# Regrouping the adaLN front of a fused block: modulation weights in stages of 256 shift and 256 scale columns, two blocks without ctx begun early, ctx turned later

## The chip, the cores and the metric

The kernel runs on one core of a Trainium2 chip. The metric is the device time of one execution in microseconds (us), lower is better. The engines are TensorE (PE; PEld is its weight load), VectorE (DVE), ScalarE (ACT), GpSimd (POOL) and SyncE (SP), which here only issues DMAs.

## The reference

Two transformer-like blocks in float32, sequence 512, width 2048. Only the start of the first one is touched:

```python
sc, scc = silu(c), silu(c_ctx)
shift, scale, gate       = split(sc  @ w_ada + b_ada, 3)      # w_ada: 2048 x 6144
shift_c, scale_c, gate_c = split(scc @ w_ada + b_ada, 3)
hc = rmsnorm(ctx, g_pre) * (1 + scale_c) + shift_c            # 256 x 2048
zc = hc @ w_in[:, :XBC_W + DT_W]                              # 4096 + 64 columns
hx = rmsnorm(x, g_pre) * (1 + scale) + shift                  # 512 x 2048
zx = hx @ w_in                                                # 12352 columns
xbc = silu(dwconv(z[..., :4096]));  ...                       # scans, MLP, w_out, second block
```

The 4096 `xbc` columns of `w_in` are sixteen blocks of 256. Blocks 0 to 11 (xh and B) are also needed for ctx; blocks 12 to 15 (C) are needed for x alone, as the last layer takes no output from ctx.

## The kernel before

Every float32 product is made from two fp32r parts (high by an ACT copy, low by a DVE subtraction), in three matmuls: high x high, high x low, low x high. So each weight piece costs one ACT and one DVE instruction of its own size before TensorE can use it.

The front computes shift and scale from the first 4096 columns of `w_ada`, loaded as 64 units of 512 KB, eight units to a stage of 512 columns. `a_unit(i)` multiplies unit `i` with silu(c), silu(c_ctx) (4 matmuls, L428, into bank 5). After the eighth, `rows_out` (DVE, L1665) copies the rows, `fold` (PE, L442) turns them to columns, `finish` (DVE) adds the bias and, after a scale stage, makes `Am` = (1 + scale) g_pre. `a_high` (ACT) and `a_low` (DVE) split the units; both names are in lines L998 and L1621, the helpers through which all ACT activations and DVE tensor-tensor operations go. The split halves have three buffers: `a_high(i)` and `a_low(i)` wait for `a used i-3`.

The order of all of it is written by hand in beats: beat `k` holds units `2k` and `2k+1` of the matmuls, while ACT and DVE split units `2k+2` and `2k+3`. `beat(k)` says what else lies in it: the fold of a stage, a tile `t` (128 of the 2048 columns) of x and ctx to be turned and modulated, and a part `sub` of the early work. `turn(t)` (L452) transposes tile `t` of the four 128-row pieces of x into bank 6, `turn_ctx(t)` (L462) that of the two pieces of ctx into bank 7. `modulate(t)` (ACT) makes `hf` and from it `HH`, the high part; `h_low` (DVE) makes `HL`. For ctx, `modulate_ctx` (DVE, L1626) makes `hf`, ACT makes `CH`, POOL makes `CL` (L2319). The rows of x and ctx (`xs`) were first squared (ACT, `junk`), given to POOL for the root, and scaled (DVE, L1625).

The early work is the product of tile `t` with the first two xbc blocks, in `t_tile` (L408 to L416): 6 matmuls of 512 columns without ctx, 6 more of 256 with it. Before, `BLOCKS` begins (0, 12): one block with ctx and one without. The 32 parts lie in beats 10 to 41; x and ctx are loaded, squared and scaled in the first eight beats; shift and scale stages alternate (`ADA_ORDER` 0, 4, 1, 5, ...), so tiles come four at a time in beats 9 to 12, 17 to 20, 25 to 28 and 33 to 36. ADA units are loaded into memory that `HH`, `HL`, `CH`, `CL` will fill (`PLACE`).

After the beats DVE splits units 8 and 9 of `w_in` and clears `zp`, `zc`; ACT may copy the finished early banks out (`zp`) only then. TensorE goes on with the other 14 blocks; the first matmul of the third block waits until banks it takes have been copied. Beside them DVE sums the rest of `w_ada` over 16 loads (`AACC`), which TensorE folds in L550, at the end of the fifth block.

Of the kernel before, what the change touches and what calls it, by code (L numbers as in the profile page):

```python
# [97 lines left out]
class Sems(dict):  # L98
# [39 lines left out]

# [230 lines left out]
def tensor_program(P, m, s, ev):  # L369
# [64 lines left out]
    def fold(st):  # L434
        P.wait_ge(*at("rowb", st))
        P.wait_ge(*at("cst"))
        if st:
            P.wait_ge(*at("mod", st - 1))
        if st >= 2:
            P.wait_ge(*at("hc", 4 * (st // 2) - 1))  # L440
        for j in range(4):
            ins = h.transpose(PB[7][:, 256 + 4 * j:260 + 4 * j], m.rowb[0:4, j * 128:(j + 1) * 128], ident[0:4, 0:4])  # L442
        ins.then_inc(*put(P.side, "fold", st))

# [10 lines left out]
    def turn_ctx(t):  # L455
        for v in range(4, 6):
            P.wait_ge(*at("xs", v))
        if t:
            P.wait_ge(*at("hc", t - 1))
        P.wait_ge(*at("mod", 2 * (t // 4) + 1))  # L460
        for v in range(2):
            ins = h.transpose(PB[7][:, v * 128:(v + 1) * 128], m.xs[4 + v][:, t * 128:(t + 1) * 128], ident)  # L462
        ins.then_inc(*put(P.side, "turn ctx", t))

    ring = deque(range(6))
    early = [[take(ring, "xbc", b, j) for j in range(3 if b < 12 else 2)] for b in BLOCKS[:2]]
    for k in range(BEATS):
        st, t, sub = beat(k)
# [4 lines left out]
        if t is not None:  # L473
            turn_ctx(t)
# [4 lines left out]
        if sub is not None:  # L479
            u, b, tt, t = early_tile(sub)  # L480
            P.wait_ge(*at("g hi", u, tt // 2))
            P.wait_ge(*at("g lo", u, tt // 2))
            first_h(t)
            tk = early[u % 2]
            ins = t_tile(m.WH[3][:, tt * 256:(tt + 1) * 256], m.WL[3][:, tt * 256:(tt + 1) * 256], t,
                         [tk[0][1], tk[1][1]], tk[2][1] if b < 12 else None)
# [501 lines left out]
def scalar_program(A, m, s, ev, I):  # L988
# [68 lines left out]
    for k in range(BEATS):  # L1057
        t = beat(k)[1]
        for i in (2 * k, 2 * k + 1):
# [4 lines left out]
            if 3 <= i < 15 and i % 2:  # L1064
                v = (i - 3) // 2
# [4 lines left out]
        sub = beat(k + 2)[2]  # L1070
# [18 lines left out]
    for i, b in enumerate(BLOCKS):  # L1089
# [12 lines left out]
        A.wait_ge(*(at("g used", 6 + i, 1) if i < 2 else at("used", 4 * i + 3)))  # L1102
# [514 lines left out]
def vector_program(V, m, s, ev):  # L1617
# [49 lines left out]
    def finish(st):  # L1667
        c = 4 * ADA_ORDER[st]
        sums = m.PB[7][:, 256:272].rearrange("p (t j) -> p t j", j=4)
# [6 lines left out]
        if st % 2:  # L1676
            p = st // 2
            V.wait_ge(*t)
            V.then(STT(m.Amv[:, 4 * p:4 * p + 4, :], m.modv[:, c:c + 4, :], 1.0,
                       m.P("g_pre", 4 * p, 4).unsqueeze(2).to_broadcast([128, 4, 2]), ALU.add, ALU.mult), "Am", p)  # L1680

    def modulate_ctx(t):
        V.wait_ge(*at("turn ctx", t))
        V.wait_ge(*at("Am", t // 4))
        if t >= 2:
            V.wait_ge(*at("CH", t - 2))
            V.wait_ge(*at("CL", t - 2))
        V.then(TS(m.hf[t % 2][:, 512:768], m.PB[7][:, 0:256], m.Amv[:, t, 1:2], m.modv[:, t, 1:2], ALU.mult, ALU.add),
               "hc", t)

    def h_low(t):
        for j in (2, 3):
            place_read(6 * (t // 4) + j)
# [3 lines left out]
    def early_low(sub):  # L1697
        u, b, tt, t = early_tile(sub)
# [767 lines left out]
def sync_program(Y, m, s, ev, I):  # L2466
# [5 lines left out]
    def ada_load(i):  # L2472
# [7 lines left out]
        load(m.aus[j], I["w_ada_s"][ADA_ORDER[i // 8] * 8 + i % 8], s.aus[j], "aus", i)  # L2480
# [26 lines left out]
    for u in range(6, 68):  # L2507
# [288 lines left out]
```

## Time and profile before

| | |
|---|---|
| median of 3 runs | 2821.99 us (2819.44 to 2822.72) |
| the profiled execution's own time | 2819.97 us |
| its span | 2818.2 us, so 1.8 us lie around it |
| PE busy | 2769.4 us, 98% |
| DVE, ACT, POOL busy | 54%, 39%, 12% |
| first tile of the early work starts | 58.55 us |
| third block starts | 170.49 us |

Busy time of matmuls is modelled with overlapping ends, so where TensorE works without a gap one instruction costs the distance from its start to the next start, which is less than its duration. The same holds for chained ACT and DVE instructions. Times in a row are us from the span's start.

### The profile page before, as it was taken

The page shows a single profiled execution, that of the slowest core. Times are in us where ns is not written, and L with a number is a line of the kernel's source. Part 1 is how long each engine was busy: PE and PEld are TensorE (multiplying, and loading weights), DVE is VectorE, ACT ScalarE, POOL GpSimd, SP SyncE. Part 2 cuts the span into 40 slices and gives each one's busy share as a digit, 9 for nine tenths or more (in the row PEclk, how much of TensorE's full clock was granted, in tenths as well). Part 3 has the DMA queues.
Part 4 walks back from the last instruction along what each step waited for, and adds up shares of the span by engine and source line. Part 5 has one row for each costly group of instructions (what it writes and reads, how often), then busy time and mean ns, then how long its engine had stood idle before and what let it go on. Part 6 is the DMA issues. An engine that isn't in the chain of part 4 may idle for free.

```text
span 2818.2 us, 33368 instructions
## 1 busy us (share of the span) xinstructions
PE 2769.4 (98%) x13174; PEld 2246.9 (80%) x13174; DVE 1529.3 (54%) x1830; ACT 1112.8 (39%) x1470; POOL 338.9 (12%) x409
## 2 busy tenths in 40 slices
PE   6999999999999999999999999899999999999999
PEld 2678888878878887888788888788878888788787
DVE  6867767765555546676753233534444434533643
ACT  7742222234343333343332332435555543432611
POOL 1011100000334223322311000100000000000000
PEclk8999999999999999999999999999999999999999
DMA  9647767754455554555455333232222223223252
GB/s 398 239 169 271 258 238 267 255 201 144 149 168 162 168 183 132 162 168 184 142 170 211 113 112 110 95 133 90 83 75 83 83 75 109 79 90 98 98 182 93
DMA packets 162122, 439.35 MB, mean 156 GB/s; under 512 B 14768, under 2 KB 59824, under 8 KB 151728
## 3 DMA queue, kind: packets, MB, share of 16 engines
q1 hardware_dynamic: 123360, 307.28, 32.8%
q0 software_dynamic: 15792, 92.99, 9.3%
q10 hardware_dynamic: 22816, 36.97, 3.7%
q8 instruction: 105, 1.72, 0.2%
q14 instruction: 49, 0.40, 0.0%
HBM read 398.11 MB, written 39.06 MB: 155 GB/s over the span
## 4 chain that ended last, share of the span: by engine, by line
PE 83%; DVE 6%; DMA 2%; ACT 2%; issue 2%; POOL 0%; ACTq 0%; DVEq 0%; SPq 0%; POOLq 0%
PE PB L408 14%; PE PB L414 14%; PE PB L413 14%; PE PB L519 10%; PE PB L520 10%; PE PB L521 10%; DMA AU<-in_w_ada 2%; DVE ca L1629 2%; DVE AACC L1629 1%; PE PB L636 1%; PE PB L653 1%; PE PB L412 1%; PE PB L411 1%; PE PB L416 1%; DVE WL L1621 1%
## 5 line engine op out<-in xcount | busy, mean ns | idle before, releaser
L1621 DVE TENSOR_TENSOR WL<-RAW,WH 128x1024 fp32r<-128x1024 f32 (+1 forms) x424 | 516.8, 1226 | 760.5 <-ACT WH L998 570.0
L408 PE MATMUL PB<-HH,WH 128*128 128x512 f32 x2048 | 815.4, 398 | 5.1 <-ACT zp L998 1.8
L414 PE MATMUL PB<-HH,WL 128*128 128x512 f32 x2048 | 801.9, 392 | 0.0
L413 PE MATMUL PB<-HL,WH 128*128 128x512 f32 x2048 | 801.2, 391 | 0.0
L998 ACT ACTIVATE WH<-RAW 128x1024 fp32r<-128x1024 f32 (+1 forms) x424 | 433.0, 1038 | 448.2 <-PE PB L521 260.7
L519 PE MATMUL PB<-WH,HH 128*128 128x512 f32 x1248 | 490.6, 393 | 0.8 <-DVE HL L1621 0.8
L521 PE MATMUL PB<-WH,HL 128*128 128x512 f32 x1248 | 486.2, 390 | 0.0
L520 PE MATMUL PB<-WL,HH 128*128 128x512 f32 x1248 | 486.1, 390 | 0.0
L408 PEld LDWEIGHTS PB<-HH,WH 128*128 128x128 f32 x2048 | 384.7, 188 | 95.7 <-issue 11.5
L414 PEld LDWEIGHTS PB<-HH,WL 128*128 128x128 f32 x2048 | 385.9, 188 | 67.0
L413 PEld LDWEIGHTS PB<-HL,WH 128*128 128x128 f32 x2048 | 386.2, 189 | 65.5 <-issue 3.1
L519 PEld LDWEIGHTS PB<-WH,HH 128*128 128x128 f32 x1248 | 234.3, 188 | 51.7 <-issue 3.4
L521 PEld LDWEIGHTS PB<-WH,HL 128*128 128x128 f32 x1248 | 234.3, 188 | 49.3
L520 PEld LDWEIGHTS PB<-WL,HH 128*128 128x128 f32 x1248 | 234.4, 188 | 48.7 <-issue 1.0
L1629 DVE SCALAR_TENSOR_TENSOR AACC<-AU,small,AACC 128x2048 f32<-128x2048 f32 x60 | 141.1, 2352 | 74.0 <-DMA AU<-in_w_ada 73.9
L2379 POOL TENSOR_TENSOR xw<-xk,wk 128x256 f32<-128x256 f32 x80 | 80.1, 1026 | 259.8 <-ACT xk L998 161.1
L412 PE MATMUL PB<-CL,WH 128*128 128x256 f32 x384 | 108.6, 283 | 0.0
L411 PE MATMUL PB<-CH,WH 128*128 128x256 f32 x384 | 107.8, 281 | 0.0
L416 PE MATMUL PB<-CH,WL 128*128 128x256 f32 x384 | 106.5, 277 | 0.0
L1629 DVE SCALAR_TENSOR_TENSOR ca<-zp,par,ca 128x512 f32<-128x512 f32 x128 | 95.8, 749 | 10.2 <-ACT ca L998 9.3
L998 ACT ACT_TABLE_LOAD x71 | 91.1, 1283 | 6.2 <-DVE wk L1621 3.5
L2291 POOL DMA_DIRECT2D g<-GT x1 | 0.5, 533 | 771.4 <-DVE Y L1621 771.4
(314 smaller groups left out, 2736.3 us busy)
## 6 DMA issues: line engine op xcount, KB each, us to landing
RAW<-in_w_in_t SPq DMA_DIRECT2D x320, 512.0 KB, 3.7
AU<-in_w_ada POOLq DMA_DIRECT2D x64, 1024.0 KB, 5.6
RAW<-in_w_out_t SPq DMA_DIRECT2D x96, 512.0 KB, 3.5
bcb<-R SPq DMA_DIRECT2D x64, 256.0 KB, 6.2
S<-so ACTq DMA_DIRECT2D x24, 384.0 KB, 2.6
ebc<-R SPq DMA_DIRECT2D x32, 256.0 KB, 6.0
SY<-evb ACTq DMA_DIRECT2D x32, 256.0 KB, 2.8
yin<-SY POOLq DMA_DIRECT2D x32, 256.0 KB, 4.2
```

Source lines behind the costliest of these rows:

```text
L408: h.matmul(banks[j], lh, m.HH[:, t, :], start=st, stop=False)
L411: h.matmul(cb, lh, m.CH[:, t, :], start=st and j == 0, stop=False, skip_group_check=True)
L412: h.matmul(cb, lh, m.CL[:, t, :], start=False, stop=False, skip_group_check=True)
L413: h.matmul(banks[j], lh, m.HL[:, t, :], start=False, stop=False)
L414: ins = h.matmul(banks[j], ll, m.HH[:, t, :], start=False, stop=en)
L416: ins = h.matmul(cb, ll, m.CH[:, t, :], start=False, stop=en, skip_group_check=True)
L519: h.matmul(bank, xh, wh[:, tt, :], start=t == 0, stop=False)
L520: h.matmul(bank, xh, wl[:, tt, :], start=False, stop=False)
L521: ins = h.matmul(bank, xl, wh[:, tt, :], start=False, stop=t == 15)
L998: return h.activation(o, a, f, **kw)
L1621: return h.tensor_tensor(o, a, b, op)
L1629: return h.scalar_tensor_tensor(out=o, in0=a, scalar=sc, in1=b, op0=op0, op1=op1)
```

## The change

- A stage of `w_ada` holds 256 shift columns and the 256 scale columns of the same tiles (`pairs` on the host, which also orders `b_ada`). `finish` makes `Am` for two tiles in every stage. `modv` is indexed by `shift_at(t)`.
- Tiles of x come two at a time after each stage: beats 5, 6, 9, 10, ..., 33, 34. ctx is turned one tile a beat in beats 20 to 35. The early parts lie in beats 6 to 37, and `BEATS` is 38 instead of 42.
- `BLOCKS` begins (12, 13), both without ctx; a loaded unit of `w_in` now holds two tiles of both blocks (`early` on the host). The ctx matmuls of one more block follow after the front.
- x pieces 0 to 3 are loaded after units 1 to 4, squared in the halves 2 to 5 of the beats and scaled in 3 to 6; ctx pieces are loaded after units 24 and 26, squared at 30 and 31 and scaled at 32 and 33.
- `fold` writes bank 4, no longer bank 7. `PLACE` follows the new order; units of `w_in` are loaded before ADA units 6, 14, ..., 62.
- The third block takes banks 4, 5, 0 instead of 5, 0, 1.

```diff
-ADA_ORDER = (0, 4, 1, 5, 2, 6, 3, 7)
-BLOCKS = (0, 12) + tuple(range(1, 12)) + (13, 14, 15)
+BLOCKS = (12, 13) + tuple(range(12)) + (14, 15)
 EARLY = 8
+SQUARED = {2: 0, 3: 1, 4: 2, 5: 3, 30: 4, 31: 5}
+SCALED = {3: 0, 4: 1, 5: 2, 6: 3, 32: 4, 33: 5}
+LOADED = {1: 0, 2: 1, 3: 2, 4: 3, 24: 4, 26: 5}
 def beat(k):
-    st = None
-    if 8 <= k <= 32 and k % 8 == 0:
-        st = k // 4 - 1
-    elif 6 <= k < 32 and k % 8 == 6:
-        st = (k - 2) // 4 - 1
-    p, r = divmod(k - 9, 8)
-    t = 4 * p + r if k >= 9 and r < 4 and p < 4 else None
-    return st, t, k - 10 if 10 <= k < 10 + 4 * EARLY else None
-BEATS = 10 + 4 * EARLY
+    st = k // 4 - 1 if k % 4 == 0 and 4 <= k <= 32 else None
+    p, r = divmod(k - 5, 4)
+    t = 2 * p + r if k >= 5 and r < 2 and p < 8 else None
+    return st, t, k - 20 if 20 <= k < 36 else None, k - 6 if 6 <= k < 6 + 4 * EARLY else None
+BEATS = 6 + 4 * EARLY
 def early_tile(s):
     u, tt = divmod(s, 4)
-    return u, BLOCKS[u % 2], tt, 4 * (u // 2) + tt
+    return u, tt % 2, tt, 2 * u + tt // 2
+def shift_at(t):
+    return 4 * (t // 2) + t % 2
...
-            ins = h.transpose(PB[7][:, 256 + 4 * j:260 + 4 * j], m.rowb[0:4, j * 128:(j + 1) * 128], ident[0:4, 0:4])
+            ins = h.transpose(PB[4][:, 4 * j:4 + 4 * j], m.rowb[0:4, j * 128:(j + 1) * 128], ident[0:4, 0:4])
...
-    early = [[take(ring, "xbc", b, j) for j in range(3 if b < 12 else 2)] for b in BLOCKS[:2]]
+    early = [[take(ring, "xbc", b, j) for j in range(2)] for b in BLOCKS[:2]]
...
-            turn_ctx(t)
+        if tc is not None:
+            turn_ctx(tc)
...
-        A.wait_ge(*at("Am", q))
+        A.wait_ge(*at("Am", t // 2))
...
+            if tc is not None and i % 2:
+                ctx_high(tc)
-            if 3 <= i < 15 and i % 2:
-                v = (i - 3) // 2
+            if i in SQUARED:
+                v = SQUARED[i]
...
-        A.wait_ge(*(at("g used", 6 + i, 1) if i < 2 else at("used", 4 * i + 3)))
+        A.wait_ge(*(at("g used", 7, 1) if i < 2 else at("used", 4 * i + 3)))
...
                 if t is not None:
-                    modulate_ctx(t)
                     h_low(t)
+                if tc is not None:
+                    modulate_ctx(tc)
...
-            if 5 <= i < 17 and i % 2:
-                v = (i - 5) // 2
+            if i in SCALED:
+                v = SCALED[i]
...
+        if i % 8 == 6:
+            raw_load(i // 8)
         ada_load(i)
-        if i % 2 and i < 12:
-            load(m.xs[i // 2], m.x_tile(I, i // 2), s.x[i // 2], "x", i // 2)
+        if i in LOADED:
+            v = LOADED[i]
+            load(m.xs[v], m.x_tile(I, v), s.x[v], "x", v)
```

## Rows read from the trace of the kernel before

**Rows 1.** Windows by stage: busy us (count) per engine, PEclk, DMA share, GB/s.

```profile
core 0: us, PE busy (x) PEld busy (x) DVE busy (x) ACT busy (x) POOL busy (x), PEclk, DMA share, GB/s
0.00:58.50 58.50, 33.13 (x108) 10.13 (x109) 38.34 (x40) 40.11 (x45) 9.21 (x19) 0.82 0.99 396
58.50:147.20 88.70, 88.22 (x458) 56.61 (x457) 72.05 (x93) 63.88 (x84) 8.26 (x11) 1.00 0.70 250
147.20:168.60 21.40, 20.12 (x109) 16.58 (x108) 12.16 (x20) 10.88 (x18) 4.88 (x6) 1.00 0.34 129
...
40.00:50.00 10.00, 8.41 (x29) 2.52 (x28) 9.54 (x12) 8.80 (x11) 2.43 (x4) 0.66 1.02 409
```

**Rows 2.** Timeline of TensorE: the first matmul of each piece of work.

```profile
58.55 0.40 PE L408 MATMUL PB<-HH,WH 128*128 128x512 f32 x1
...
60.66 0.60 PE L452 MATMUL PB<-cst,xs 128*128 128x128 f32 x4
...
63.16 0.40 PE L408 MATMUL PB<-HH,WH 128*128 128x512 f32 x1
...
110.68 0.40 PE L428 MATMUL PB<-WH,scs 128*4 128x512 f32 x1
...
112.53 0.39 PE L408 MATMUL PB<-HH,WH 128*128 128x512 f32 x1
...
113.92 0.39 PE L428 MATMUL PB<-WH,scs 128*4 128x512 f32 x1
...
146.84 0.40 PE L442 MATMUL PB<-cst,rowb 4*128 4x4 f32 x4
147.17 0.50 PE L408 MATMUL PB<-HH,WH 128*128 128x512 f32 x1
...
170.49 0.47 PE L408 MATMUL PB<-HH,WH 128*128 128x512 f32 x1 [1.80 <-ACT zp L998]
```

**Rows 3.** DMA from 25 to 60 us, and a landing on ACT's timeline.

```profile
DMA packets 3659, 14.38 MB, mean 411 GB/s; under 512 B 406, under 2 KB 406, under 8 KB 3401
...
22.66 1.06 ACT L998 ACTIVATE WH<-aus7HH 128x1024 fp32r<-128x1024 f32 x1 [0.21 <-DMA aus7HH<-in_w_ada_s]
```

**Rows 4.** Timeline of ACT: square, split, modulation.

```profile
42.57 1.90 ACT L998 ACTIVATE junk<-xs 128x2048 f32<-128x2048 f32 x1
...
44.46 1.05 ACT L998 ACTIVATE WH<-aus16CH 128x1024 fp32r<-128x1024 f32 x1
...
66.24 0.76 ACT L998 ACTIVATE hf<-PB,small 128x512 f32<-128x512 f32 x1
67.03 0.63 ACT L998 ACTIVATE HH<-hf 128x512 fp32r<-128x512 f32 x1
```

**Rows 5.** Timeline of DVE: scaling, ctx modulation, low parts, rows, splits.

```profile
44.09 1.28 DVE L1625 TENSOR_SCALAR xs<-xs,small 128x2048 f32<-128x2048 f32 x1
...
63.44 0.54 DVE L1626 TENSOR_SCALAR hf<-PB,small 128x256 f32<-128x256 f32 x1
63.90 0.69 DVE L1621 TENSOR_TENSOR HL<-hf,HH 128x512 fp32r<-128x512 f32 x1
64.50 0.67 DVE L1665 COPY rowb<-PB 4x512 f32<-4x512 f32 x1
...
138.20 1.22 DVE L1621 TENSOR_TENSOR WL<-aus19HH,WH 128x1024 fp32r<-128x1024 f32 x1
139.34 1.22 DVE L1621 TENSOR_TENSOR WL<-aus22CH,WH 128x1024 fp32r<-128x1024 f32 x1
```

**Rows 6.** DVE, then ACT, at the end of the front.

```profile
164.92 2.36 DVE L1621 TENSOR_TENSOR WL<-RAW,WH 128x1024 fp32r<-128x1024 f32 x2 [0.33 <-ACT WH L998]
167.35 0.51 DVE L1736 MEMSET zp<- 128x544 f32 x1
...
169.02 0.60 ACT L998 ACTIVATE zp<-PB 128x512 f32<-128x512 f32 x1 [3.25 <-DVE zc L1737]
```

**Rows 7.** What TensorE waited for over the whole kernel: total, times, longest.

```profile
PE PB L408 <- ACT zp L998: 1.8, 1, 1.8
...
PE PB L550 <- DVE AACC L1629: 1.1, 1, 1.1
```

More of the change, by code:

```diff
@@ L479, in tensor_program @@
         if sub is not None:
-            u, b, tt, t = early_tile(sub)
+            u, i, tt, t = early_tile(sub)
             P.wait_ge(*at("g hi", u, tt // 2))
             P.wait_ge(*at("g lo", u, tt // 2))
-            first_h(t)
-            tk = early[u % 2]
+            P.wait_ge(*at("HH", t))
+            P.wait_ge(*at("HL", t))
             ins = t_tile(m.WH[3][:, tt * 256:(tt + 1) * 256], m.WL[3][:, tt * 256:(tt + 1) * 256], t,
-                         [tk[0][1], tk[1][1]], tk[2][1] if b < 12 else None)
+                         [bank for b, bank in early[i]])
             if tt % 2:
@@ L1057, in scalar_program @@
     for k in range(BEATS):
-        t = beat(k)[1]
+        st, t, tc, sub = beat(k)
         for i in (2 * k, 2 * k + 1):
@@ L1069, in scalar_program @@
                 junk = A.then(act(m.junk, m.xs[v], ACT.Square, acc=m.ss[:, v:v + 1]), "x squared", v)
-        sub = beat(k + 2)[2]
+        sub = beat(k + 2)[3]
         if sub is not None and sub % 2 == 0:
@@ L1675, in finish @@
         t = V.then(TT(m.modv[:, c:c + 4, :], m.modv[:, c:c + 4, :], sums[:, :, 2:4], ALU.add), "mod", st)
[L1676 to L1680, printed above, removed]
+        V.wait_ge(*t)
+        V.then(STT(m.Amv[:, 2 * st:2 * st + 2, :], m.modv[:, c + 2:c + 4, :], 1.0,
+                   m.P("g_pre", 2 * st, 2).unsqueeze(2).to_broadcast([128, 2, 2]), ALU.add, ALU.mult), "Am", st)
     def modulate_ctx(t):
         V.wait_ge(*at("turn ctx", t))
-        V.wait_ge(*at("Am", t // 4))
+        V.wait_ge(*at("Am", t // 2))
         if t >= 2:
@@ L1687, in modulate_ctx @@
             V.wait_ge(*at("CL", t - 2))
-        V.then(TS(m.hf[t % 2][:, 512:768], m.PB[7][:, 0:256], m.Amv[:, t, 1:2], m.modv[:, t, 1:2], ALU.mult, ALU.add),
-               "hc", t)
+        V.then(TS(m.hf[t % 2][:, 512:768], m.PB[7][:, 0:256], m.Amv[:, t, 1:2], m.modv[:, shift_at(t), 1:2],
+                  ALU.mult, ALU.add), "hc", t)
     def h_low(t):
-        for j in (2, 3):
-            place_read(6 * (t // 4) + j)
+        place_read(6 * (t // 4) + 2 + t % 4 // 2)
         V.wait_ge(*at("HH", t))
@@ L1711, in vector_program @@
             finish(beat(k - 1)[0])
-        t = beat(k)[1]
+        st, t, tc, sub = beat(k)
         for i in (2 * k, 2 * k + 1):
@@ L2501, in sync_program @@
     for i in range(64):
-        if i >= 16 and i % 8 == 0:
-            raw_load(i // 8 - 2)
+        if i % 8 == 6:
+            raw_load(i // 8)
         ada_load(i)
-        if i % 2 and i < 12:
-            load(m.xs[i // 2], m.x_tile(I, i // 2), s.x[i // 2], "x", i // 2)
-    for u in range(6, 68):
+        if i in LOADED:
+            v = LOADED[i]
+            load(m.xs[v], m.x_tile(I, v), s.x[v], "x", v)
+    for u in range(8, 68):
         raw_load(u)
@@ L2742 @@
     bc = lambda a: np.broadcast_to(a.reshape(1, -1), (128, a.size))
+    pairs = np.arange(4096).reshape(2, 8, 256).transpose(1, 0, 2).reshape(-1)
     parts = {
@@ L2766 @@
     first = pack(flat(xbc[:, BLOCKS]), 4, 256)
-    w_in_t = np.concatenate([first[[0, 4, 1, 5, 2, 6, 3, 7]], first[8:], pack(flat(zs), 4, 256), pack(flat(vv), 2, 512),
+    early = first[:8].reshape(2, 4, 128, 2, 2, 256).transpose(1, 3, 2, 4, 0, 5).reshape(8, 128, 1024)
+    w_in_t = np.concatenate([early, first[8:], pack(flat(zs), 4, 256), pack(flat(vv), 2, 512),
                              pack(flat(uz), 4, 256)])
@@ L2778 @@
         "x": v["x"], "ctx": v["ctx"], "w_ada": v["w_ada"], "w_ada_2": v["w_ada_2"],
-        "w_ada_s": pack(v["w_ada"][0][:, :4096], 2, 512),
+        "w_ada_s": pack(v["w_ada"][0][:, pairs], 2, 512),
         "w_in_t": w_in_t, "w_dt": w[:, 4096:4160].reshape(16, 128, 64).transpose(1, 0, 2).reshape(128, 1024),
```

39 lines of the change are left out of this document (19 added, 20 removed).

## The prediction

> **What bounds the kernel now.** I read the page first: TensorE is busy for 98% of the span, so after the front a microsecond counts only if TensorE loses or gains it. Then the windows by stage, to see where it isn't busy [rows 1]: in the first 58.5 us it is busy for 33 us, and that figure is flattered by the granted clock (0.82 on the mean, 0.66 from 40 to 50 us); from 58.5 to 147.2 us it has no gap, with DVE at 81% and ACT at 72%; then a tail. DMA is full until some 80 us (0.99 up to 58.5 us) and at 0.70 behind that. So the opening is set by what arrives, the middle by TensorE with DVE close behind it, the tail by short chains from engine to engine. The change leaves TensorE's total work alone. What it can move is TensorE's lost time before the third block, which starts at 170.49 us [rows 2], and what that does to waits behind it [rows 7].
>
> **Prices, as distances between starts** [rows 2]. Two ADA units take 112.53 - 110.68 = 1.85 us, one 0.93. A tile without ctx takes 113.92 - 112.53 = 1.39, one with ctx 60.66 - 58.55 = 2.11. From 60.66 to 63.16 lie two units and both turnings, so these cost 2.50 - 1.85 = 0.65, by their number of transposes (4 and 2) 0.43 for x, 0.22 for ctx. A fold takes 0.33, and some 0.1 more in the next matmul. On DVE [rows 5]: a split 1.14, `hf` of ctx 0.46, `HL` 0.60, the row copy 0.6, scaling 1.2, three small operations of `finish` some 0.5, half a unit of w_in some 0.6 (my estimate, from `HL`, which has its shape). On ACT [rows 4]: a square with its read-out 1.89, a split 0.95 (1.05 less the overlap), `hf` 0.79, `HH` 0.6.
>
> **The ledger before.** Work of the front on TensorE: 64 x 0.93 + 16 x 2.11 + 16 x 1.39 + 16 x 0.65 + 8 x 0.43 = 59.5 + 33.8 + 22.2 + 10.4 + 3.4 = 129.3 us. The third block starts at 170.5, so 41.2 are lost. Up to 58.55: 22 units, two tiles turned, two folds, 20.5 + 1.3 + 0.9 = 22.7 of work, 35.9 lost. From there to the last fold's end at 147.17: 42 units, 12 and 10 tiles, 10 turnings, 5 folds are 39.1 + 25.3 + 13.9 + 6.5 + 2.2 = 87.0 in 88.6, 1.6 lost. Tail to 170.49: 2 + 4 tiles without, 4 with ctx, 4 turnings, 8.3 + 8.4 + 2.6 = 19.3 in 23.3, 4.0 lost. The sum is 41.5, which closes.
>
> **The ledger after.** The work in the front is 16 x 0.72 = 11.5 us less, and exactly this comes back behind it, as ctx matmuls of block 0. It is worth nothing either way. So I only count lost time.
>
> *Opening.* 512 KB land each 1.27 us (411 GB/s) [rows 3]. At 22.66 the 14th piece was in (units 0 to 7, and three 1 MB pieces of x that count double). With x first, unit 4 is piece 11 (18.9 us), unit 5 piece 14 (22.7), unit 6, behind a unit of w_in, piece 16 (25.2). ACT then has behind unit 4 a chain of its own: square 0, unit 5 until 23.7, square 1, unit 6, square 2, unit 7, square 3: the last square ends at 31.3, 4 us behind the DMA. The root on POOL takes 1.3, DVE splits unit 8 and scales piece 3 until 34.7, copies the rows of stage 0 (35.3), unit 9 until 36.5, fold at 38, two splits and half of w_in until 39.5, `finish` 40.0, ACT `hf` and `HH` 41.5, `HL`, unit 13 until 43.8; the first tile starts at 44.9. TensorE is partly at 0.66 of its clock here (40 to 50 us) [rows 1], so I take 45.5. Work until then: 14 units, 2 turnings of x, 1 fold, 14.3. Lost 31.2, against 35.9: a gain of 4.7.
>
> The Trainium skill (TensorE: Matmul & The Clock Gate, Part 1) has the throttled clock as the default and activity as what releases it. By that rule the first tiles are done at half rate, where the tiles of before found the full clock. The trace agrees that the level is low before the tiles and 1.00 in them [rows 1]; what it costs is a rival below.
>
> *Beats 7 to 14.* Four beats ask TensorE for 7.4 + 5.6 + 0.9 + 0.4 = 14.3 us. DVE has 9.1 + 1.2 + 1.2 + 0.6 + 0.5 = 12.6. TensorE bounds; for hand-overs that are not yet settled I put 0.5.
>
> *Beats 15 to 17.* Squaring and scaling of ctx came free in the DMA-bound opening; now they lie where all engines are busy. ACT has in beat 15 two splits and two squares, 1.9 + 3.8 = 5.7 us in a beat of 3.6; DVE behind it 2.3 + 2.4 + 0.6 = 5.3, and behind those the `finish` on which `Am` of tiles 6 and 7 hangs. Followed step by step (split 33 behind square 4, split 34 behind square 5 at +5.7, two DVE splits and two scalings, half of w_in, `finish`, `hf`, `HH`, the ACT split, the DVE split), unit 37 is ready 4.9 us later than in the pattern of the beats before. About 0.6 of slack takes off some: 4.3 lost. At least nothing, if the three split buffers carry it; at most the whole 3.8 + 2.4 = 6.2.
>
> *Beats 20 to 31.* Now ctx is turned in every beat. TensorE: 14.3 + 0.9 = 15.2 in four beats. DVE: 12.6 + 4 x 0.46 = 14.4, and in each beat with x it waits for `HH` behind ACT, which itself has waited for `Am`. I get 16.0 for four beats by following them, 0.8 lost in each of three rounds: 2.5. Before, 1.6 were lost in the middle. Least 0, most 5.
>
> *Tail.* The last fold comes about 145. `finish` stands in DVE's order behind half a unit of w_in, which waits for ACT's half, so `Am` comes 2.4 behind the fold (before 1.6). Then tile 14 and 15 have `hf`, `HH`, `HL`, and ctx tile 13, 14, 15 each wait for `hf` of the one before, in the same order on PE. By these steps the last ctx tile is on DVE at 155.4, ACT and POOL make its parts until 156.8, DVE splits units 8 and 9 until 159 and clears `zp` (1.6 us). ACT's first copy ends at 161.4 and the third block starts at 161.5. In the trace, splits, clearing and copy also stand in this order before the third block [rows 6]. The last fold to the third block are 16.4 for 9.9 of work; TensorE's later release of ACT and DVE adds 0.7: 7.2 lost, against 4.0. So 3.2 are given back. Least -1 (the third block needs one bank that ACT empties, not two), most 6.
>
> *Behind.* The two first convolutions have no ctx half, 8 x 0.4 = 3.2 us less on DVE ahead of the first AACC sum. POOL's loads start relatively later, but DVE is what they wait for. The 1.1 us of L550 [rows 7] should go. Least 0, most 2.5 gained.
>
> Sum: -4.7 + 0.5 + 4.3 + (2.5 - 1.6) + 3.2 - 1.1 = +3.1 us. The traced execution took 2819.97, the median is 2821.99; the difference is within the spread of the three runs. I add to the median: 2825.1 us. The third block should start at about 170.5 - 11.5 + 4.2 = 163.2.
>
> **The rivals.**
> - *The opening's gain stays.* For it: DVE is at 81% and ACT at 72% before, and three split buffers even out a burst. Then bump and ctx beats lose 1.5 together and the tail 1: -4.7 + 0.5 + 1.5 - 1.6 + 1 - 1.1 = -4.4, 2817.6 us. It is faster than the 0.2% if the first tile also starts at 44 or earlier: -7, 2815. Against it: both engines have the same work in 3.6 us beats as they had in 4.0. Chance 0.3, of which 0.15 beyond 0.2%.
> - *DVE becomes the bound.* If DVE's waits for `HH` and for ACT grow to 0.5 us a beat from beat 20, these beats lose 6, and the bump isn't absorbed at all: -4.7 + 0.5 + 6 + 4.4 + 3.2 - 1.1 = +8.3, 2830 us. It decides as soon as four beats take over 16.5 us. For it: in four beats with x and ctx DVE has 14.4 of 15.2. Chance 0.18.
> - *The clock.* Tiles and units in the first 6 us of early work at 1.2 GHz take twice as long; 3 us on top, +6.1, 2828. For it the 0.66 [rows 1], against it that TensorE then has more work than before. Chance 0.1.
> - *It does nothing*, as the waits only change their names: part of my forecast.
>
> **How the numbers follow.** Forecast 0.42, around 2825 with 2821 to 2829 as its own range. 0.2% are 5.6 us, about what a measurement of this kernel can tell from no change: faster means under 2816.4, slower over 2827.6. Slower gets 0.18 of DVE, 0.05 of the clock and 0.07 of the forecast's upper end, 0.3; faster 0.16; the same 0.54. For 8 in 10 the range goes from 2815 to 2832.
>
> **What would show it.** The first L408 near 45.5 us, not 58.5; a gap of some 4 us in TensorE near 78 to 92 us, with ACT `junk` and DVE `xs` in it; four beats at 16 us and not 15.2 behind that; the third block at 163; no wait at L550. I am wrong if the third block starts before 158 or behind 167, or if a unit of `w_ada` arrives late in the second half, since `PLACE` leaves only four units between the last uses of a buffer.

## The result and the profile after

The changed kernel takes 2825.61 us (median of 20 runs), the one before 2819.55 (20 runs on the same chip): ratio 1.0018, 95% interval 1.0011 to 1.0025. These are 3.1 to 7.0 us more. The ratio is within the 0.2% that count as no change, close to the upper edge, and the interval reaches beyond it. The forecast was 2825.1, in the chance given 0.54. But it was +3.1 us on 2821.99, a median of three runs that stood high; against the longer series the step is +6.06, twice the forecast one. That the two times lie only 0.5 us apart is luck: the base stood 2.4 us high and the step came out 3.0 us too small.

The profiled execution took 2825.90 us with a span of 2824.1, against 2819.97 and 2818.2: +5.9. The windows by stage of the changed kernel, cut where its own stages end (columns as in [rows 1]), and of the stretch behind:

```profile
core 0: us, PE busy (x) PEld busy (x) DVE busy (x) ACT busy (x) POOL busy (x), PEclk, DMA share, GB/s
0.00:45.50 45.50, 22.27 (x68) 6.45 (x69) 25.04 (x26) 27.42 (x33) 5.54 (x14) 0.77 0.98 390
45.50:145.60 100.10, 93.87 (x447) 54.27 (x446) 90.37 (x113) 79.08 (x102) 17.73 (x15) 1.00 0.73 276
145.60:165.10 19.50, 13.41 (x65) 9.55 (x63) 10.79 (x20) 8.37 (x15) 4.85 (x7) 1.00 0.32 106
165.10:168.60 3.50, 3.47 (x11) 2.99 (x12) 2.24 (x3) 1.87 (x3) 0.00 (x0) 0.51 1.02 427
```

Against [rows 1], the opening is 13 us shorter and the middle has DVE at 90% (before 81%). TensorE is at 94% in that middle, where it had no gap before. The tail has 6 us without a matmul. And the last row has something that was nowhere in the forecast: TensorE is busy, but at a granted clock of 0.51 of the full one, so at 1.2 GHz for nearly all of it and not at 2.4.

The timeline of TensorE shows where its time is lost (the counterpart of [rows 2]; L413 is the line of the tiles here, L433 that of the units, L445 the fold; the bracket is the idle time before, and who ended it):

```profile
45.62 0.39 PE L413 MATMUL PB<-HH,WH 128*128 128x512 f32 x1
...
81.18 0.40 PE L433 MATMUL PB<-WH,scs 128*4 128x512 f32 x1 [0.81 <-DVE WL L1628]
...
86.36 0.39 PE L433 MATMUL PB<-WH,scs 128*4 128x512 f32 x1 [0.81 <-DVE WL L1628]
...
89.40 0.66 PE L456 MATMUL PB<-cst,xs 128*128 128x128 f32 x4 [0.59 <-ACT hf L1001]
...
92.50 0.40 PE L433 MATMUL PB<-WH,scs 128*4 128x512 f32 x1 [1.51 <-DVE WL L1628]
...
147.68 0.40 PE L445 MATMUL PB<-cst,rowb 4*128 4x4 f32 x4
...
153.63 0.44 PE L465 MATMUL PB<-cst,xs 128*128 128x128 f32 x2 [1.25 <-DVE hf L1633]
...
156.59 0.44 PE L465 MATMUL PB<-cst,xs 128*128 128x128 f32 x2 [1.13 <-DVE hf L1633]
...
165.13 0.79 PE L413 MATMUL PB<-HH,WH 128*128 128x512 f32 x1 [3.69 <-ACT zp L1001]
...
167.21 0.63 PE L413 MATMUL PB<-HH,WH 128*128 128x512 f32 x1
```

By the ledger of the prediction and with its prices:

| | lost before | forecast | measured |
|---|---|---|---|
| up to the first tile (58.55; 45.62) | 35.9 | 31.2 | 31.3 |
| to the end of the last fold (147.17; 148.01) | 1.6 | 7.3 | 8.7 |
| to the third block (170.49; 165.13) | 4.0 | 7.2 | 7.2 |

148.01 is the last fold at 147.68 and 0.33 for it. The middle is 102.4 us for 93.7 of work, the tail 17.1 for 9.9; with 14.3 in the opening that is 117.9 us of work, 11.4 less than before. The third block starts 5.36 us earlier with these 11.4 still to be done: 6.0 us lost, where the forecast had 4.2.

Behind it, TensorE before waited 1.1 us at L550 [rows 7], twice (1.7 in all, at 187.94 and 569.70) for DVE's `WL`, and 0.65 for a load at L667:

```profile
187.94 0.47 PE L408 MATMUL PB<-HH,WH 128*128 128x512 f32 x1 [0.37 <-DVE WL L1621]
...
569.70 0.47 PE L408 MATMUL PB<-HH,WH 128*128 128x512 f32 x1 [1.32 <-DVE WL L1621]
...
777.26 1.50 PE L667 MATMUL PB<-cst,xT 128*128 128x128 f32 x12 [0.65 <-DMA xT<-S]
```

The changed kernel has none of these. So 3.5 us of waits are gone in this pair of traces, where the forecast had 1.1. Against this stands the clock. A half tile with ctx takes 1.05 us further on, and the first two behind the third block's start take 2.17 in the kernel before (170.49 to 172.66), at the full clock. Here they take 2.08 (to 167.21) and 1.67 (to 168.88), 3.75 in all, so 1.6 us are lost to the clock. Another 2 us or so are in the rate of all tiles; e11 and e12 are about that.

### The profile page after: what moved, and what is told of

It is laid out like the page before. It is cut to its first block, busy times and chain, and to the rows that moved or that the text cites. A ratio compares the mean times of both kernels' runs of the same rounds, so it can differ in the third digit from the quotient of the medians.

```text
span 2824.1 us, 33335 instructions
## 1 busy us (share of the span) xinstructions
PE 2772.1 (98%) x13174; PEld 2245.8 (80%) x13174; DVE 1530.3 (54%) x1834; ACT 1112.1 (39%) x1470; POOL 343.0 (12%) x409
## 4 chain that ended last, share of the span: by engine, by line
PE 91%; DVE 3%; ACT 3%; issue 2%; DMA 1%; POOL 0%; SPq 0%; DVEq 0%; ACTq 0%
PE PB L413 16%; PE PB L418 15%; PE PB L419 15%; PE PB L522 10%; PE PB L523 10%; PE PB L524 10%; PE PB L416 2%; PE PB L417 2%; PE PB L421 2%; ACT WH L1001 1%; PE PB L639 1%; PE PB L656 1%; PE PB L433 1%; DVE WL L1628 1%; PE PB L886 1%
## 5 line engine op out<-in xcount | busy, mean ns | idle before, releaser
L413 PE MATMUL PB<-HH,WH 128*128 128x512 f32 x2048 | 818.9, 400 | 4.1 <-ACT zp L1001 3.7
L413 PEld LDWEIGHTS PB<-HH,WH 128*128 128x128 f32 x2048 | 385.0, 188 | 93.7 <-issue 7.8
L1001 ACT ACTIVATE zp<-PB 128x512 f32<-128x512 f32 x32 | 18.9, 603 | 209.7 <-PE PB L421 187.6
```

Source lines behind the costliest of these rows:

```text
L413: h.matmul(banks[j], lh, m.HH[:, t, :], start=st, stop=False)
L1001: return h.activation(o, a, f, **kw)
```

## The experiments

Each is an edit of the changed kernel unless it says that it is one of the kernel before. Ratios are against the kernel before, run on the same chip (its median 2819.50 us for e1 to e4, 2820.02 for e5 to e8, 2820.35 for e9 to e12). Each kernel has 11 executions (e7: 10; e11 and e12: one), and its ratio is good to about 0.1%, so I read the third block's start in the trace first and the median second. As the chips differ, a "median gain" over the changed kernel is its 6.06 us above the kernel before, less what the variant has above the kernel before on its own chip. "Third block" is the start of the third block; the changed kernel has 165.13. "Four beats" is the distance from one fold to the next.

**e1: the norm of ctx cut small.** The two ctx pieces are squared and scaled over 8 columns only (so the norm of ctx is left out of the computation), the order of everything stays.

```diff
+cols = slice(0, 2048 if v < 4 else 8)   # v: piece; square and scaling take [:, cols]
```

> The changed kernel with the squares and the scaling of the two ctx pieces cut from 2048 to 8 columns (the rest of ctx is left unscaled, so the work left out is 2 squares of 1.89 us on ACT and 2 scalings of 1.2 us on DVE, in beats 15 and 16). Theory: these four instructions alone open the four gaps of TensorE between 81 and 92.5 us (0.81 + 0.81 + 0.59 + 1.51 = 3.7 us), so the gaps go, the third block starts 3.5 to 4.5 us earlier than 165.1, and the kernel takes 3.5 to 4.5 us less than the changed one, about 1.5 to 2 more than the one before. Rival, DVE is the bound in the whole middle: the gaps only move to the beats behind, the third block comes under 2 us earlier.

Measured: 2821.15 us, 1.0001 (0.9992 to 1.0010); third block 160.76, 4.37 us earlier. The four gaps between 81 and 93 us are gone; what TensorE waited for between 60 and 180 us in this kernel (total, times, longest):

```profile
PE PB L413 <- ACT zp L1001: 3.7, 1, 3.7
PE PB L465 <- DVE hf L1634: 2.4, 2, 1.3
PE PB L433 <- DVE rowb L1673: 1.5, 2, 0.8
PE PB L433 <- DVE WL L1629: 0.9, 3, 0.3
```

In the changed kernel `WL` has 4.1 there. The forecast put 4.3 on this step; the run gives 4.4 at the third block, and 4.4 in the median. It is shown, place and price.

**e4: modulation of ctx cut small.** `modulate_ctx` writes 8 of 256 columns from tile 2 on, which takes the 0.46 us of DVE out of each ctx beat (the ctx half of these tiles is then not modulated).

```diff
-TS(m.hf[t % 2][:, 512:768], m.PB[7][:, 0:256], ...)
+TS(m.hf[t % 2][:, 512:520], m.PB[7][:, 0:8], ...)
```

> The changed kernel with ctx tiles 2 to 15 modulated by DVE in 8 columns instead of 256 (the other 248 columns keep what the tiles before left), which takes some 0.4 us from DVE in each beat from 22 to 35; ACT, POOL and TensorE do what they did. Theory: DVE is what costs four beats 16.8 us where TensorE needs 15.2 (folds at 100.2, 116.9, 133.7, 147.7); then they come down to 15.2 to 15.5, the tail gets 0.5 to 1 shorter, and in all 3 to 4.5 us go. Rival, the loop from TensorE to ACT to DVE and back (hf, HH, HL, split) sets the beat, with DVE's work only a part of it: under 1.5 us go.

Measured: 2822.61 us, 1.0005 (0.9996 to 1.0014); third block 162.95, 2.2 us earlier, and a median gain of 3.0. Four beats take 16.4 and 16.2 us, where the changed kernel takes 16.7 and 16.8 (folds at 100.22, 116.93, 133.73, 147.68). With 1.8 us less for DVE in four beats, only 0.3 and 0.6 came out, 1.15 up to the last fold and 1.0 in the tail. The expected 15.2 to 15.5 did not come; the whole lies between the theory (3 to 4.5 us) and the rival (under 1.5). If DVE's volume were the bound, four beats would have come down to the 15.2 that TensorE needs. So the volume isn't the main cause of the 16.8; e9 asks whether the order is.

**e9: `finish` before the half unit of w_in.** The three small operations that make `Am` move from the start of the next beat to ahead of `early_low`.

```diff
 # beat k of DVE
-        if beat(k - 1)[0] is not None:
-            finish(beat(k - 1)[0])
...
+        if st is not None:
+            finish(st)
         # behind it: the low part of half a unit of w_in
```

> The changed kernel with one amendment: DVE does finish in the beat of the fold, ahead of the low part of half a unit of w_in, and not at the start of the next beat. Nothing is left out and DVE's work is the same. Theory: what makes four beats with ctx 16.7 to 16.8 us long is the loop fold, finish, hf, HH, split, matmul, in which finish waits behind ACT's half unit, and not the amount of DVE's work; then four beats come down to 15.9 us, as they were with the three amendments together, the last fold is at 145 to 146, and the tail is 0.5 to 1.5 shorter: third block near 161.5, kernel 3 to 4 us under the changed one. Rival, the shorter beats of the run with three amendments came from the spread squares: four beats stay at 16.7 and under 1.5 us go.

Measured: 2823.05 us, 1.0008 (0.9999 to 1.0017); third block 161.13, 4.0 us earlier. The timelines of DVE around the fold at 100 us, the changed kernel first, then this one:

```profile
100.56 1.20 DVE L1628 TENSOR_TENSOR WL<-aus21HL,WH 128x1024 fp32r<-128x1024 f32 x1
101.79 1.13 DVE L1628 TENSOR_TENSOR WL<-RAW,WH 128x512 fp32r<-128x512 f32 x1
102.84 0.15 DVE L1628 TENSOR_TENSOR small<-PB,par 128x8 f32<-128x8 f32 x1
...
105.11 0.69 DVE L1628 TENSOR_TENSOR HL<-hf,HH 128x512 fp32r<-128x512 f32 x1 [0.55 <-ACT HH L1001]
```

```profile
99.62 1.20 DVE L1628 TENSOR_TENSOR WL<-aus21HL,WH 128x1024 fp32r<-128x1024 f32 x1
100.75 0.15 DVE L1628 TENSOR_TENSOR small<-PB,par 128x8 f32<-128x8 f32 x1
...
101.37 0.68 DVE L1628 TENSOR_TENSOR WL<-RAW,WH 128x512 fp32r<-128x512 f32 x1
...
103.36 0.69 DVE L1628 TENSOR_TENSOR HL<-hf,HH 128x512 fp32r<-128x512 f32 x1 [0.17 <-ACT HH L1001]
```

In the changed kernel `finish` stands 1.23 + 1.05 us behind the start of its split, in this one right behind it; DVE then waits 0.17 us for `HH` and not 0.55. Folds come at 99.26, 115.18, 131.08 and 144.41: four beats take 15.9 us. Of the 4.0 us, 1.0 is gained before the first of these folds, 2.3 in the ctx beats, 0.7 in the tail; the median gain is 3.4. DVE has the same instructions, so it is their order, and not their number, that makes four beats longer than the 16.0 of the forecast. The order has two effects here, and the run does not separate them: `Am` comes earlier, and the half unit's `WL` between them took 1.13 us beside an operation of POOL and takes 0.68 behind it (see the last section). Of six such halves between 100 and 145 us all take 1.13 to 1.23 in the changed kernel, and three in this one.

**e3: only the borders cleared.** The third block's `zp` and `zc` are cleared in their two border columns at either side, not whole, the rest is overwritten anyway.

```diff
-V.then(h.memset(m.zp[i], 0.0))
-V.then(h.memset(m.zc[i], 0.0), ...)
+V.then(h.memset(m.zp[i][:, :, 0:2], 0.0))
+V.then(h.memset(m.zp[i][:, :, 66:68], 0.0))
+V.then(h.memset(m.zc[i][:, 0:2], 0.0))
+V.then(h.memset(m.zc[i][:, 258:260], 0.0), ...)
```

> The changed kernel with zp and zc cleared only in the border columns that the copies don't fill (eight memsets of 2 or 16 columns in place of four of 260 and 544). Nothing else moves. Theory: the chain splits of units 8 and 9, clearing, ACT copy, third block is what ends the front, so the third block starts 1.0 to 1.4 us earlier than 165.1; and if the gap of 3.7 us before it is what drops TensorE to 1.2 GHz (granted clock 0.50 from 165 to 168.5), a gap of 2.4 us may or may not keep the clock: with the clock kept, 1.6 us more. So 1 to 3 us less than the changed kernel. Rival, the third block waits for something else (POOL or the loads): no change.

Measured: 2822.74 us, 1.0008 (0.9999 to 1.0017); third block 163.67 after a gap of 2.15, and the granted clock there stayed at 1.00. DVE at the end of the front in the changed kernel (the counterpart of [rows 6]):

```profile
160.31 2.36 DVE L1628 TENSOR_TENSOR WL<-RAW,WH 128x1024 fp32r<-128x1024 f32 x2 [1.50 <-ACT WH L1001]
162.74 0.51 DVE L1741 MEMSET zp<- 128x544 f32 x1
163.25 0.28 DVE L1742 MEMSET zc<- 128x260 f32 x1
...
```

1.46 us of the 1.6 us of clearing come out at the third block: the chain splits, clearing, copy by ACT, third block is the one that the prediction named. As the clock does not fall, this saves the 1.6 us behind it as well: 1.46 + 1.6 = 3.1, and the median gain is 2.8.

**e2: the banks in the old order.** The third block takes banks 5, 0, 1 as in the kernel before, and so waits for two copies. The question was whether the choice of banks makes the tiles behind it slower (see e11 and e12).

```diff
+if i == 1: ring.rotate(-1)
```

> The changed kernel with the ring of banks turned by one before the third block, so that it takes banks 5, 0, 1 as in the kernel before, and no longer 4, 5, 0; nothing is left out. Half a tile with ctx takes 1.055 us in the changed kernel and 1.047 in the one before, which over 384 of them are some 2 to 3 us that no wait shows. Theory A: it is the choice of banks; then half a tile is back at 1.047 and the kernel is about 2 us faster, though the third block now waits for two copies and starts some 0.8 us later. Theory B: it is not the banks (a chance phase of this program, or of the chip); then half a tile stays at 1.055 and the time goes up by the 0.8 us of the second copy.

Measured: 2826.05 us, 1.0018 (1.0009 to 1.0026); third block 165.60 after a gap of 4.20, 0.5 later (0.8 expected), and the tiles stayed slow. So the banks don't make the tiles slow, and the new order of banks is worth 0.5 us at the third block.

**e5: the kernel before with a longer gap.** `zp` is cleared five times where it was cleared twice, and each clearing waits for the last, so that DVE is done some 2 us later ahead of the third block.

```diff
 # the kernel before
+for i in range(5):
+    w = V.then(h.memset(m.zp[i % 2], 0.0))
+    V.wait_ge(*w)
 for i in range(2):
-    V.then(h.memset(m.zp[i], 0.0))
```

> The kernel before, with zp cleared five times where it was cleared twice (each clearing waits for the last), so that the third block starts some 2 us later; nothing is left out. In the changed kernel and in three of four variants TensorE stood still for 3.4 to 4.2 us there, had granted clock 0.50 for some 3 us after it, and from then on took 1.053 us or more for half a tile with ctx; in the kernel before (gap 1.8) and with borders only (2.15) the clock stayed at 1.00 and half a tile took 1.047. Theory A: the gap causes both, so here the gap of 3.8 to 4.0 us brings 2.1 us of itself, 1.6 of the clock and 2 of the slower tiles, 5 to 6 us in all, over 2824.5. Theory B: the slower tiles belong to the changed kernel's order: then the tiles stay at 1.047 and it is 3.5 us at most. Theory C: neither, 2 us.

Measured: 2822.11 us, 1.0008 (0.9999 to 1.0017); third block 172.86 instead of 170.49, after a gap of 4.13. Now the kernel before shows the low clock too (one row of the windows, columns as above; the granted clock is the third number from the end):

```profile
172.80:176.30 3.50, 3.44 (x11) 2.99 (x12) 2.04 (x4) 2.61 (x5) 0.00 (x0) 0.50 0.02 5
```

So the longer gap brings the clock down with no other part of the change. Its first three half tiles take from 172.86 to 178.48, 5.62 us, where they take 3.23 in the kernel before at the full clock: 2.4 us more. 2.4 of gap and 2.4 of clock, less 1.1 for the wait at L550, which is gone here as well, would give 3.7; the spans differ by 3.4, the medians by 2.1, which is what the third theory had ("neither") and which the trace contradicts. Half a tile takes 1.0533 us here up to 293 us and 1.0467 from 297.8 on, so slow tiles don't stay behind such a gap.

**e6: squares of x cut small**, 8 of 2048 columns for the four x pieces (the norm of x is then a sum over 8 columns).

```diff
+cols = slice(0, 8 if v < 4 else 2048)   # v: piece; the square takes [:, cols]
```

> The changed kernel with the squares of the four x pieces cut from 2048 to 8 columns (the factors of the norm are then wrong; left out are four ACT instructions of 1.89 us in the first 31 us). Theory: ACT's chain of splits and squares, and not the DMA, sets when stage 0 is done, so the first tile starts near 38 to 40 us and not at 45.6, and as TensorE is full from there on, the kernel takes 5 to 7 us less than the changed one. Rival, the DMA sets it: unit 9 is in at 29 us, so fold and first tile move by less than 2 us.

Measured: 2824.34 us, 1.0009 (1.0001 to 1.0018); first tile at 44.08 and not 38 to 40, third block 164.04. 7.6 us less of ACT gave 1.5 at the first tile (the rival had "under 2", for the DMA). My account of the opening as one chain of ACT is wrong here. Behind ACT stands DVE, almost without a pause from 24.85 to 37.5 us with splits and all four scalings. ACT's split at 35.24 waits 2.35 us for matmuls of TensorE, and those had waited 2.27 us for DVE's row copy. TensorE has a granted clock of 0.50 from 24 to 31.4 us and again from 34.9 to 41.7:

```profile
24.85 1.28 DVE L1633 TENSOR_SCALAR xs<-xs,small 128x2048 f32<-128x2048 f32 x1
...
33.27 0.67 DVE L1673 COPY rowb<-PB 4x512 f32<-4x512 f32 x1
```

```profile
34.00 0.39 PE L433 MATMUL PB<-WH,scs 128*4 128x512 f32 x1 [2.27 <-DVE rowb L1673]
```

```profile
35.24 1.06 ACT L1001 ACTIVATE WH<-aus14HL 128x1024 fp32r<-128x1024 f32 x1 [2.35 <-PE PB L433]
```

**e7: ctx loaded, squared and scaled early**, as in the kernel before (loads after units 5 and 6, squares in halves 6 and 7, scalings in 8 and 9).

```diff
-SQUARED = {2: 0, 3: 1, 4: 2, 5: 3, 30: 4, 31: 5}
-SCALED = {3: 0, 4: 1, 5: 2, 6: 3, 32: 4, 33: 5}
-LOADED = {1: 0, 2: 1, 3: 2, 4: 3, 24: 4, 26: 5}
+SQUARED = {2: 0, 3: 1, 4: 2, 5: 3, 6: 4, 7: 5}
+SCALED = {3: 0, 4: 1, 5: 2, 6: 3, 8: 4, 9: 5}
+LOADED = {1: 0, 2: 1, 3: 2, 4: 3, 5: 4, 6: 5}
```

> The changed kernel with ctx loaded behind units 5 and 6, squared in halves 6 and 7 and scaled in 8 and 9, right behind x, as it was before; the rest of the change stays. Theory: the gaps of TensorE between 81 and 92.5 us (3.7 us, 4.4 in the folds) go, but two squares on ACT (3.8 us) and two pieces of DMA (5 us, ahead of units 6 on) fall into the opening, so that the first tile starts near 49.5 us and not at 45.6. In all within 1.5 us of the changed kernel. Rival, ACT and DMA have the slack in the opening: first tile within 1 us of 45.6, kernel 4 us faster than the changed one.

Measured: 2827.41 us, 1.0026 (1.0017 to 1.0035); first tile at 52.56, 7 us later and not 4, no gaps between 78 and 92 us, third block 168.88. Later ctx costs 4.4 us in the middle (e1) and earns 7 in the opening. At the third block the net is 3.75, more than the 2.6 of these two, because here the first tile met the low clock, as the third rival of the prediction had it:

```profile
52.56:55.70 3.14, 3.14 (x9) 2.02 (x8) 2.95 (x3) 1.57 (x3) 0.00 (x0) 0.50 1.04 414
```

Half a tile takes 1.28 us there and 0.68 in the changed kernel, and the next fold comes 8.0 us behind the first tile and not 6.8. The median is 1.3 us above the changed kernel's, so loading ctx later is a part of the change that pays.

**e10: the kernel before with only the borders cleared** (the edit of e3).

> The kernel before, with zp and zc cleared in their borders only; nothing is left out. Theory: the clearing stands on the chain to the third block here as well, so 1.4 us go (third block at 169.0), and the 1.1 us wait at L550 may grow by as much, since the sums over w_ada start with POOL and DVE and not with TensorE: 0 to 1.4 us less than before in all. So the border clearing alone doesn't explain that the version with three amendments is faster than the kernel before. Rival: 3 us or more go, and the order of the front has no part in it.

Measured: 2819.25 us, 0.9997 (0.9988 to 1.0006); third block 169.0 after a gap of 0.31. It gives the kernel before 1.1 us, within the interval of no change. The wait at L550, which was expected to grow, is gone in this execution.

**e8: three repairs together.** The edits of e9 and e3, and the norm of ctx spread over more beats:

```diff
-SQUARED = {..., 30: 4, 31: 5}
-SCALED = {..., 32: 4, 33: 5}
+SQUARED = {..., 22: 4, 30: 5}
+SCALED = {..., 24: 4, 32: 5}
```

> The changed kernel with three amendments, nothing left out: the squares of ctx in halves 22 and 30 and the scalings in 24 and 32, so that no two fall together; finish before the last half unit's low part instead of behind it, so Am doesn't wait for ACT's part; zp and zc cleared in their borders only. Theory: the two squares are taken up by the three split buffers but for about 1 us, 3.4 us back; Am of tiles 14 and 15 comes 2 us earlier in the tail, 1.5 to 2 back; borders 1.5 back, and the clock and the rate of the tiles as in the run with borders alone, 3 more. Third block near 158 to 159, kernel 2815 to 2817, so faster than the one before by 0.1 to 0.2%. Rival: DVE is so full that each saved wait reappears in the next beat; then third block over 161 and the kernel not under 2819.

Measured: 2815.6 us, 0.9983 (0.9974 to 0.9992), a median gain of 10.5 us over the changed kernel and 4.4 under the one before; third block 157.85, 7.28 us earlier. e9 and e3 alone give 4.0 and 1.46 of that, so by subtraction the spread gives 1.8 and not the 3.4 expected; it was not run alone. What TensorE waited for up to 180 us, without the opening:

```profile
PE PB L413 <- ACT zp L1001: 2.2, 1, 2.2
PE PB L465 <- DVE hf L1633: 1.9, 2, 1.1
PE PB L433 <- DVE WL L1628: 1.7, 2, 0.9
PE PB L433 <- DVE rowb L1672: 0.9, 2, 0.4
```

```profile
157.85:161.00 3.15, 3.15 (x17) 2.75 (x18) 1.91 (x3) 1.84 (x3) 0.00 (x0) 1.00 1.00 423
```

Its gap is 2.17 us and the clock stays. It leaves nothing out; it is the version that beats both, by 0.17% against the kernel before.

**e11 and e12: the changed kernel and the one before once more**, one execution each, side by side.

> The changed kernel once more, unaltered, for a second look at half a tile with ctx. Theory A: the rate of the tiles behind the front (1.0533 against 1.0467 us) belongs to the execution and not to the program; then it may come out at 1.0467 here, with a span near 2822, and two levels 2 us apart are to be seen in the times of one kernel. Theory B: it belongs to the program, and is 1.0533 again.

> The kernel before once more, unaltered. Theory A (the rate belongs to the execution): 1.0467 or 1.0533 us for half a tile, by chance. Theory B (to the program): 1.0467 again.

Measured: own times 2826.26 and 2820.68, spans 2824.4 and 2818.9. They were to say whose the slower tiles are. In the first pair of traces nearly every half tile with ctx took longer in the changed kernel. The first matmul of such half tiles, 29 of them apart: the kernel before, the changed one, and e12:

```profile
299.76 0.39 PE L408 MATMUL PB<-HH,WH 128*128 128x512 f32 x1
...
330.11 0.39 PE L408 MATMUL PB<-HH,WH 128*128 128x512 f32 x1
```

```profile
299.76 0.40 PE L413 MATMUL PB<-HH,WH 128*128 128x512 f32 x1
...
330.31 0.40 PE L413 MATMUL PB<-HH,WH 128*128 128x512 f32 x1
```

```profile
299.80 0.40 PE L408 MATMUL PB<-HH,WH 128*128 128x512 f32 x1
...
330.34 0.40 PE L408 MATMUL PB<-HH,WH 128*128 128x512 f32 x1
```

30.35 / 29 = 1.0466 us in the first, 30.55 / 29 = 1.0534 in the second, 30.54 / 29 = 1.0531 in e12, which is the kernel before. So the slower rate is not a mark of the changed kernel.

It does not belong to a whole execution either. e11, the changed kernel, has the quicker rate between 191.77 and 222.12 (30.35 / 29) and the slower one from 269 us on:

```profile
191.77 0.39 PE L413 MATMUL PB<-HH,WH 128*128 128x512 f32 x1
...
222.12 0.39 PE L413 MATMUL PB<-HH,WH 128*128 128x512 f32 x1
...
300.05 0.40 PE L413 MATMUL PB<-HH,WH 128*128 128x512 f32 x1
...
330.60 0.40 PE L413 MATMUL PB<-HH,WH 128*128 128x512 f32 x1
```

In all 14 traces the rate stays as it is until TensorE does something else in between, and may be another one behind that. It fell from 1.053 to 1.047 at the wait at 187.94 in the kernel before, and at the last fold of `AACC` (near 278 to 296 us) in e3, e5, e6, e7, e8 and e9; in the kernel before it rose at the first of these folds and fell again at the last; it rose at the first (268.2 us) in e11. It stayed at 1.0533 throughout in the changed kernel, e1, e2, e4, e10 and e12. At 0.0067 us each, the 384 half tiles with ctx behind the third block's start (352 in the kernel before) make 2.6 us (2.4) if all are slow.

e12 also shows the low clock (0.55 from 170.40 to 174.00, 1.5 us lost) after a gap of 1.82 us, and only one of the four waits behind it, 0.7 us at L667. What each of the four profiled executions of the two kernels loses behind the start of the third block, in us:

| | clock | slower tiles | waits | sum |
|---|---|---|---|---|
| before, first trace | 0 | 0.2 | 3.5 | 3.7 |
| before, e12 | 1.5 | 2.4 | 0.7 | 4.6 |
| changed, first trace | 1.6 | 2.6 | 0 | 4.2 |
| changed, e11 | 2.5 | 1.9 | 0.3 | 4.7 |

Where TensorE is slower, the engines that it waited for have caught up. Like against like, the changed kernel's first trace and e12 are both slow throughout and both have the low clock. Their spans differ by 5.2 us, those of e11 and e12 by 5.5, and the ledger up to the third block says -5.36 + 11.4 = 6.0. So nearly all of the difference of the two kernels is made before the third block; the three terms behind it add up to about as much in the one as in the other.

## Why the prediction was right, and where it was not

- **Opening: right.** First tile 45.62 for 45.5, gain 4.6 for 4.7. Its reasoning was right only in part. The chain of squares on ACT was followed as if it alone set the pace; e6 shows that DVE's splits and scalings stand 1.5 us behind it. And the 0.6 us added for a clock of 0.66 from 40 to 50 us were put at a place where the changed kernel has 1.00 (39.00 to 45.60); its low clock lies before, at 18 to 39 us, where two units take from 35.27 to 38.6 and not 1.85 us. That the sum came out is partly luck.
- **The clock on the first tiles: did not happen.** Tiles have the full clock from 45.62 (0.39 us a matmul, 0.68 a half tile). The rival was no idle one: in e7 the first tile came at 52.56 and met 0.50. The Trainium skill's rule (TensorE: Matmul & The Clock Gate, Part 1) was weighed at the wrong place. The trace agrees with it at another, the third block: the level was 1.00, TensorE stood for 3.69 us, and the clock was at 0.51 when work came back.
- **Beats 15 to 17: right.** Forecast 4.3, shown by e1 as 4.4. The burst of 5.7 us on ACT and the `finish` behind it were followed instruction by instruction.
- **Beats 7 to 14 and 20 to 31: too small.** Forecast 0.5 and 2.5, measured together 8.7 - 4.4 = 4.3. Four beats with ctx took 16.7 and 16.8 us and not 16.0. From the fold at 100.22 to that at 147.68 are 47.5 us for 43.8 of work, so 3.7 lost in these beats and 0.6 in the ones before. By the prediction's own sign, four beats over 16.5 us, this is the rival "DVE becomes the bound"; its 6 us over-sized the price, and it sums wrongly, as it leaves out the 1.6 us that were lost before. Its mechanism, DVE's waits for `HH` behind `Am`, is near to what the runs show. But the order of the work does more than the volume: e4 takes DVE's volume and wins some 0.4 of 1.8 us in four beats, e9 leaves it, changes the order, and wins 0.9. The prediction had `finish` behind half a unit of w_in, but priced the half at 0.6 us; with ctx beside it, it took 1.05 from start to start. How much of the 0.7 us is that price and how much the steps followed is not shown.
- **Tail: right.** 7.2 for 7.2, and e3 shows the end of its chain. Its absolute times (last fold at 145, third block at 161.5) were 1.2 and 1.7 us ahead of what the prediction's own ledger gives. One bank in place of two, its lower bound of -1, is worth 0.5 us by e2.
- **Behind: the wait at L550 went, as said, but more is there.** Three more waits, 2.4 us, went as well, and the clock and the slower tiles took 4.0 us. In the second pair (e11 and e12) neither kernel waits at L550. So the 1.1 us that were to be gained are not shown.
- **The step that was missing.** The ledger counted each gap as its own length. The gap at the third block grew from 1.80 to 3.69 us, and the clock behind it cost 1.6 more; e5 shows that in the kernel before such a gap does the same.

Against the first pair of traces: the forecast was +3.1. The middle adds 1.4, the opening and rounding 0.4, the clock 1.6, the slower tiles 2.4, and the waits take off another 2.4, sum 6.5; the spans differ by 5.9 and the medians by 6.1. The ledger gives some 0.5 us too much in the other two pairs as well; I can't place them. What stays open besides is why the tiles have the one or the other rate, and what makes the two groups in which the times of one kernel fall (e3: 2820.9 to 2822.7 and 2824.1 to 2826.2; e8: 2814.9 to 2816.0 and 2817.9 to 2818.4): only one execution of each was profiled.

## What to carry over

Moving cheap work out of a DMA-bound opening doesn't make it free elsewhere: price it in the beat where it lands, as it stands in the queues of the two helper engines there, and spread it (e8) before you judge the move. When a short chain feeds a whole stage (three operations of 0.16 us that make `Am`), its place in the queue of a busy engine can be worth more than the volume: here 0.9 us in four beats against 0.4 for 1.8 us less of work on that engine. List what stands ahead of it. A stall of TensorE that grows costs more than its length once the clock falls behind it: e3 shortened one by 1.5 us and gained about 3. And before a small difference of two profiles is put down to a change, profile each kernel once more: here single terms of 1 to 3 us came and went between executions of one kernel.

## What the runs showed of the hardware that was not expected

- **The clock after a stall.** TensorE stood before the third block 3.4 to 4.2 us in nine traces (the changed kernel, e1, e2, e4 to e7, e9, e11), and in all nine the granted clock of the next 3.5 us was 0.50 to 0.60, that is 1.2 GHz for most of them. After 2.15, 2.17 and 0.31 us (e3, e8, e10) it was 1.00; after 1.8 us it was 1.00 once (the kernel before) and 0.54 once (e12). The cost on top of the gap was 1.3 to 2.7 us, and 1.6 and 2.5 in two executions of the same changed kernel.
- **Two rates of the same tile** at a granted clock of 1.00, 1.0467 and 1.0533 us, that change within one execution: each lasts until TensorE waits or folds in between, and may be another one behind it.
- **DVE and POOL take turns.** The subtraction that makes half a unit's `WL` on DVE takes 0.69 us alone and 1.22 when it starts while POOL makes a `CL`, which in turn takes 1.18 and not 0.73. DVE, then POOL, in the changed kernel:

```profile
87.32 0.69 DVE L1628 TENSOR_TENSOR WL<-RAW,WH 128x512 fp32r<-128x512 f32 x1
...
143.70 1.21 DVE L1628 TENSOR_TENSOR WL<-aus23CL,WH 128x1024 fp32r<-128x1024 f32 x1
144.84 1.22 DVE L1628 TENSOR_TENSOR WL<-RAW,WH 128x512 fp32r<-128x512 f32 x1
```

```profile
144.32 1.18 POOL L2324 TENSOR_TENSOR CL<-hf,CH 128x256 fp32r<-128x256 f32 x1 [2.73 <-ACT CH L1001]
147.04 0.73 POOL L2324 TENSOR_TENSOR CL<-hf,CH 128x256 fp32r<-128x256 f32 x1 [1.54 <-ACT CH L1001]
```

POOL's operation starts at 144.32, inside DVE's of 143.70 to 144.91, and ends at 145.50, 0.59 behind it; DVE's next starts at 144.84 and ends at 146.06, 0.56 behind POOL's. So each seems to stand until the other has finished. The Trainium skill (SBUF — State Buffer, Who interferes with whom) says that a DVE instruction with two inputs in SBUF contends with a GpSimd instruction that reads SBUF, as its second input comes through the read interface that the two share, and calls that an exclusive lock. The trace agrees; at some 0.5 us each time it belongs in the price of DVE's beats with ctx, where I had put none.
